# Sums of the keys' squares from two rounded parts, placed behind both query products, in a two-layer hybrid decoder kernel

## The reference, cut to what matters

```
def mla(c_q, c_kv, k_rope, ...):
    q = (rms_norm(c_q, cq_g) @ w_uq).reshape(b_, t_, MLA_HEADS, QK_HEAD)
    ckv = rms_norm(c_kv, ckv_g)
    k_nope = (ckv @ w_uk).reshape(b_, t_, MLA_HEADS, QK_NOPE)
    v = (ckv @ w_uv).reshape(b_, t_, MLA_HEADS, V_HEAD)
    k = jnp.concatenate([k_nope, k_r], axis=-1)
    q = rms_norm(q, qn_g)
    k = rms_norm(k, kn_g)          # needs the sum of k_nope's squares per head and token
    ... rope on the last 64 entries, causal softmax(q k) v
```

## Time and profile before

| what | us |
|---|---|
| median of three executions (range) | 1718.37 (1717.32 to 1718.63) |
| the profiled execution, its own time | 1717.03 |
| its span, first to last instruction | 1715.2 |
| PE busy (share of the span) | 1698.3 (99%) |
| PE weight loads | 1593.6 (93%) |
| POOL busy | 1203.0 (70%) |
| DVE busy | 892.2 (52%) |
| ACT busy | 484.9 (28%) |
| mean granted TensorE clock | 0.998 of full |

### The profile page before, as it was taken

The page is one execution under the profiler, slowest core; times in us unless marked ns, Lnnn a source line. Parts: engine busy times, 40 slices in busy tenths (PEclk is TensorE's granted clock), DMA queues, the critical chain, the costliest instruction groups (busy, mean ns, idle before and its releaser), DMA issues.

```text
span 1715.2 us, 32297 instructions
## 1 busy us (share of the span) xinstructions
PE 1698.3 (99%) x11976; PEld 1593.6 (93%) x11976; DVE 892.2 (52%) x1279; ACT 484.9 (28%) x867; POOL 1203.0 (70%) x1365
## 2 busy tenths in 40 slices
PE   7999999999999999999999999999999999999999
PEld 7999999999999999999999999999998888888887
DVE  7966758485545452212358757584856455322221
ACT  4423333332322331101134333333324223311110
POOL 7764848485688777777765748484857898777773
PEclk9999999999999999999999999999999999999999
DMA  4431222122232232232432313121222222322233
GB/s 158 139 98 62 92 72 81 65 92 86 87 110 74 86 123 100 86 98 86 162 116 76 107 59 98 60 92 66 92 86 98 98 86 86 139 96 98 88 121 112
DMA packets 49408, 164.23 MB, mean 96 GB/s; under 512 B 6048, under 2 KB 7456, under 8 KB 49056
## 3 DMA queue, kind: packets, MB, share of 16 engines
q1 hardware_dynamic: 41328, 146.56, 25.8%
q10 hardware_dynamic: 8032, 17.03, 3.0%
HBM read 152.21 MB, written 10.81 MB: 95 GB/s over the span
## 4 chain that ended last, share of the span: by engine, by line
PE 97%; DVE 1%; ACT 0%; issue 0%; ACTq 0%; POOL 0%; DVEq 0%; POOLq 0%
PE slots L507 85%; PE slots L572 3%; PE slots L605 3%; PE slots L667 2%; PE slots L590 1%; PE slots L541 1%; PE slots L557 1%; PE slots L575 0%; ACT residual_or_merged L955 0%; DVE sc_acc L1393 0%; DVE sc_acc L1397 0%; DVE residual_or_merged L1347 0%; PE slots L550 0%; DVE r_bias L1337 0%; DVE norm_diag L1103 0%
## 5 line engine op out<-in xcount | busy, mean ns | idle before, releaser
L419 POOL TENSOR_TENSOR w_lo<-w_raw,w_hi 128x256 fp32r<-128x256 f32 x1004 | 838.3, 865 | 20.9
L414 POOL TENSOR_SCALAR w_hi<-w_raw 128x1024 fp32r<-128x1024 f32 x251 | 289.5, 1154 | 337.0 <-PE slots L507 329.9
L507 PE MATMUL slots<-h_hi,w_hi 128*128 128x264 f32 (+1 forms) x2112 | 521.3, 311 | 0.0
L507 PE MATMUL slots<-h_lo,w_hi 128*128 128x264 f32 (+1 forms) x2112 | 515.6, 308 | 0.0
L507 PE MATMUL slots<-h_hi,w_lo 128*128 128x264 f32 (+1 forms) x2112 | 514.7, 308 | 0.0
L507 PEld LDWEIGHTS slots<-h_hi,w_hi 128*128 128x128 f32 x2112 | 342.7, 188 | 19.7
L507 PEld LDWEIGHTS slots<-h_hi,w_lo 128*128 128x128 f32 x2112 | 341.7, 188 | 19.1
L507 PEld LDWEIGHTS slots<-h_lo,w_hi 128*128 128x128 f32 x2112 | 342.0, 188 | 17.8
L507 PE MATMUL slots<-branch_hi,w_hi 128*128 128x264 f32 (+1 forms) x576 | 144.0, 313 | 10.5 <-DVE branch_lo L1109 8.7
L507 PE MATMUL slots<-branch_lo,w_hi 128*128 128x264 f32 (+1 forms) x576 | 142.9, 312 | 0.0
L507 PE MATMUL slots<-branch_hi,w_lo 128*128 128x264 f32 (+1 forms) x576 | 142.5, 311 | 0.0
(11 more groups left out here) (236 smaller groups left out, 2860.6 us busy)
## 6 DMA issues: line engine op xcount, KB each, us to landing
w_raw<-w_units SPq DMA_DIRECT2D x251, 512.0 KB, 3.3
stream<-sc_acc ACTq DMA_DIRECT2D x16, 264.0 KB, 2.1
sc_back<-stream SPq DMA_DIRECT2D x2, 2112.0 KB, 8.0
x_old<-stream SPq DMA_DIRECT2D x16, 264.0 KB, 4.3
stream<-residual_or_merged ACTq DMA_DIRECT2D x16, 264.0 KB, 2.4
ab_raw<-w_units SPq DMA_DIRECT2D x8, 512.0 KB, 4.2
residual_or_merged<-xt ACTq DMA_DIRECT2D x4, 528.0 KB, 7.9
stream<-xt ACTq DMA_DIRECT2D x1, 2112.0 KB, 9.5
```

The lines of the kernel that those rows point to most:

```text
L414: pool.tensor_scalar(hi, raw, 1.0, 1.0, ALU.mult, ALU.mult).then_inc(sem("hi_part"), 1)
L419: op = pool.tensor_tensor(lo[:, cols], raw[:, cols], hi[:, cols].bitcast(F32), ALU.subtract)
L507: mm = pe.matmul(out[:, a_, 0:t1 - t0], w(k), x(k)[:, t0:t1], start=(n == 0), stop=(n == 3 * ks - 1))
```

## The change

In the sums of the keys' squares the fp32 squares are replaced by a rounded hi part and a rounded lo part, and the matrix of ones by a rounded one (`ones_r`, made once). ACT squares each key twice, once into fp32 (`ct[4]`, `ct[5]`) and once rounded into `kn_hi`, which is not in use at that point; DVE subtracts to get the lo part in `kn_lo`. PE makes each sum from four fp32r matmuls where there were two fp32 ones. The sums stand behind both query products on PE; on ACT the square roots stand behind the queries' parts; on DVE the queries' lo parts stand ahead of the reading of the sums. `sc_input(0)` moves up on DVE, to the place between the keys' and the rotary lo parts. The gaps of filling k-tiles are dealt anew, 28 in place of 24 ahead of the first scores. Slots stay as they were. The new semaphores' entries and the making of `ones_r` on ACT at the start are left out of this diff.

```diff
@@ -71,7 +71,7 @@
 FILL = ("c0", "x0", "g0", "b0", "ga0", "c1", "x1", "g1", "b1", "ga1")
-FILLS = (8, 16, 4, 4, 4, 5, 5, 2, 6, 6, 7, 7, 6)
+FILLS = (8, 20, 4, 4, 3, 4, 5, 3, 5, 5, 6, 7, 6)
 STAGES = {"NORM": (1, 0, 0), "CQ": (1, 6, 2), "ATT": (4, 12, 0), "RG": (4, 8, 0), "MR": (4, 4, 0),
@@ -83,7 +83,7 @@
     "ATT": [("va", 2, "att_mm"), ("kn0", 0, "att_mm"), ("kn1", 1, "att_mm"), ("vb", 3, "unit_used"),
-            ("sum_k0", 0, "att_mm"), ("sum_k1", 1, "att_mm"), ("qn0", 2, "att_mm"), ("qn1", 3, "unit_used"),
+            ("qn0", 2, "att_mm"), ("qn1", 3, "unit_used"), ("sum_k0", 0, "att_mm"), ("sum_k1", 1, "att_mm"),
             ("qr", 1, "att_mm"), ("stat_q", 3, "att_mm"),
...
@@ -676,17 +677,26 @@
 
-                    for h in range(2):
-                        out = free("ATT", l, p, f"sum_k{h}")
-                        pe.wait_ge(*at("k_squared", l, p, h + 1))
-                        spread_sum(out, ct[h]).then_inc(sem("att_mm"), 1)
-
                     pe.wait_ge(*was_read("CQ", l, 0, "q2"))
                     hi, lo = unit_ready("ATT", l, p, 1)
-                    for h in range(2):
+
+                    def queries(h):
+
                         out = free("ATT", l, p, f"qn{h}")
...
                                 KQ).then_inc(sem("unit_used" if h else "att_mm"), 1)
+
+                    queries(0)
+                    queries(1)
+                    for h in range(2):
+                        out = free("ATT", l, p, f"sum_k{h}")
+                        pe.wait_ge(*at("k_sq_lo", l, p, h + 1))
+                        for a_ in range(2):
+                            cols = slice(a_ * HALF, (a_ + 1) * HALF)
+                            for n, squares in enumerate((kn_hi, kn_lo)):
+                                mm = pe.matmul(out[:, a_, 0:HALF], ones_r[:], squares[:, h, cols], start=(n == 0),
+                                               stop=(n == 1))
+                        mm.then_inc(sem("att_mm"), 1)
                     out = free("ATT", l, p, "qr")
@@ -824,6 +834,7 @@
             act.activation(ident_r[:], ident[0:TOK, 0:TOK], ACT.Copy).then_inc(sem("consts_ready"), 1)
+            act.activation(ones_r[:], ones[:], ACT.Copy).then_inc(sem("consts_ready"), 1)
             act.activation(causal_r[:], causal[0:TOK, 0:TOK], ACT.Copy).then_inc(sem("consts_ready"), 1)
@@ -888,24 +899,26 @@
                         act.wait_ge(*ready("ATT", l, p, f"kn{h}"))
-                        act.activation(halves(ct[h][:]), slot(slot_of("ATT", f"kn{h}")), ACT.Square).then_inc(
+                        act.activation(halves(ct[4 + h][:]), slot(slot_of("ATT", f"kn{h}")), ACT.Square).then_inc(
                             sem("k_squared"), 1)
+                        act.activation(halves(kn_hi[:, h, :]), slot(slot_of("ATT", f"kn{h}")), ACT.Square).then_inc(
+                            sem("k_sq_hi"), 1)
                         act.activation(halves(ct[2 + h][:]), slot(slot_of("ATT", f"kn{h}")), ACT.Identity, bias=zero,
...
                     for h in range(2):
-                        act.wait_ge(*was_read("ATT", l, p, f"sum_k{h}"))
-                        act.activation(ct[4 + h][:], ct[4 + h][:], ACT.Sqrt, bias=eps, scale=1.0 / QK).then_inc(
-                            sem("k_rms"), 1)
-
-                    for h in range(2):
                         act.wait_ge(*ready("ATT", l, p, f"qn{h}"))
...
                                        scale=hparam(l, QN_G)).then_inc(sem("q_hi"), 1)
+                    for h in range(2):
+                        act.wait_ge(*was_read("ATT", l, p, f"sum_k{h}"))
+                        act.activation(ct[4 + h][:], ct[4 + h][:], ACT.Sqrt, bias=eps, scale=1.0 / QK).then_inc(
+                            sem("k_rms"), 1)
+
                     act.wait_ge(*ready("ATT", l, p, "qr"))
@@ -916,6 +929,8 @@
                         act.wait_ge(*at("k_full", l, p, h + 1))
+                        if h == 0:
+                            act.wait_ge(*ready("ATT", l, p, "sum_k1"))
                         act.activation(kn_hi[:, h, :], ct[2 + h][:], ACT.Copy).then_inc(sem("k_hi"), 1)
@@ -1252,6 +1267,15 @@
                     for h in range(2):
+                        dve.wait_ge(*at("k_squared", l, p, h + 1))
+                        dve.wait_ge(*at("k_sq_hi", l, p, h + 1))
+                        lo_part(kn_lo[:, h, :], ct[4 + h][:], kn_hi[:, h, :], "k_sq_lo")
+                    for g in range(2):
+                        dve.wait_ge(*at("q_hi", l, p, g + 1))
+                        dve.scalar_tensor_tensor(halves(qn_lo[:, g, :]), slot(slot_of("ATT", f"qn{g}")),
+                                                 hparam(l, QN_G), halves(qn_hi[:, g, :]).bitcast(F32), ALU.mult,
+                                                 ALU.subtract).then_inc(freed("ATT", f"qn{g}"), 1)
+                    for h in range(2):
                         dve.wait_ge(*ready("ATT", l, p, f"sum_k{h}"))
@@ -1265,11 +1289,6 @@
                         k_inverse(g)
-
-                        dve.wait_ge(*at("q_hi", l, p, g + 1))
-                        dve.scalar_tensor_tensor(halves(qn_lo[:, g, :]), slot(slot_of("ATT", f"qn{g}")),
-                                                 hparam(l, QN_G), halves(qn_hi[:, g, :]).bitcast(F32), ALU.mult,
-                                                 ALU.subtract).then_inc(freed("ATT", f"qn{g}"), 1)
 
@@ -1300,9 +1319,17 @@
                                                      freed("ATT", "stat_q") if h else sem("q_ms"), 1)
+                    def sc_input(s):
+
+                        dve.wait_ge(*ready("ATT", l, p, f"x{s}"))
+                        dve.wait_ge(*was_read("ATT", l, p, f"c{s}"))
+                        dve.tensor_tensor(halves(s_pad[:, SCONV - 1:]), slot(slot_of("ATT", f"x{s}")),
+                                          halves(s_c[:]), ALU.mult).then_inc(freed("ATT", f"x{s}"), 1)
+
                     for h in range(2):
...
                         lo_part(kn_lo[:, h, :], ct[2 + h][:], kn_hi[:, h, :], "k_lo")
+                    sc_input(0)
                     for h in range(2):
@@ -1377,13 +1404,6 @@
 
-                    def sc_input(s):
-
-                        dve.wait_ge(*ready("ATT", l, p, f"x{s}"))
-                        dve.wait_ge(*was_read("ATT", l, p, f"c{s}"))
-                        dve.tensor_tensor(halves(s_pad[:, SCONV - 1:]), slot(slot_of("ATT", f"x{s}")),
-                                          halves(s_c[:]), ALU.mult).then_inc(freed("ATT", f"x{s}"), 1)
-
                     def sc_conv(s, m):
@@ -1418,7 +1438,6 @@
 
-                    sc_input(0)
                     for n in range(10):
```

More of the change, by code:

```diff
@@ L112 @@
     "rope_split": ("ATT", 1), "att_mm": ("ATT", 10),
-    "k_squared": ("ATT", 2), "v_hi": ("ATT", 2), "k_sum": ("ATT", 1), "k_rms": ("ATT", 2), "q_summed": ("ATT", 2), "k_rinv": ("ATT", 2), "k_full": ("ATT", 2), "kr_scaled": ("ATT", 2),
+    "k_squared": ("ATT", 2), "k_sq_hi": ("ATT", 2), "k_sq_lo": ("ATT", 2), "v_hi": ("ATT", 2), "k_sum": ("ATT", 1), "k_rms": ("ATT", 2), "q_summed": ("ATT", 2), "k_rinv": ("ATT", 2), "k_full": ("ATT", 2), "kr_scaled": ("ATT", 2),
     "k_hi": ("ATT", 2), "k_lo": ("ATT", 2), "krp_hi": ("ATT", 2), "krp_lo": ("ATT", 2),
@@ L215, in build @@
         ones = sb("ones", [P, P])
+        ones_r = sb("ones_r", [P, P], F32R)
         lane_consts = sb("lane_consts", [P, 2 + 2 * NTOK])
@@ L650, in _ @@
                     pe.wait_ge(sem("params_in"), 48)
-                    pe.wait_ge(sem("consts_ready"), 2)
+                    pe.wait_ge(sem("consts_ready"), 3)
                 with nc.Fori(0, PAIRS, engines=bass.OrderedEngineSet([pe.engine]), head_slot={pe.engine: 0}) as p:
```

## The result

| | before | after |
|---|---|---|
| median (range), us | 1717.84 (1715.89 to 1718.63) | 1821.76 (1821.02 to 1822.43) |
| span of the profiled execution, us | 1715.2 | 1820.1 |
| mean granted TensorE clock | 0.998 | 0.975 |

The change makes the kernel slower by 6.05%, ratio 1.0605 with a 95% interval of 1.0589 to 1.0621. The forecast was slower, 1737 us with a range of 1728 to 1749; the direction held, and the size was missed by 85 us.

A forecast was written before the change was run, and what follows sets the result against it. PE was taken to bound the kernel, with no slack. -7.4 + 0.8 + 20.6 + 4 = +18.0 us on 1717.03 gives 1735.0; 1736.4 for a median, plus half a microsecond for the clock: 1737, range 1728 to 1749.

The forecast's parts named there:

- PE's own work: Key sums on PE: eight fp32r matmuls take 0.98 us in place of 1.90, -0.92 a pass, -7.4 over eight.
- Anything that takes work off PE is gained whole: Premise: PE is busy 1698.3 of 1715.2 us, so saved work counts whole and new waits are lost whole.
- The wait for `vb`'s slot: Ahead of `qn1`: PE waits some 0.1 us a pass (0 to 0.3) for DVE's read, +0.8 over eight.
- The wait ahead of `qr`: PE waits for DVE to read `sum_k1` in the shared slot 1: 2.6 us a pass, 20.6 over eight.
- DVE's chain and the first scores: Normed keys begin 3.9 us later, at 264.9; PE reaches the first scores at 282.7, with no wait taken.
- the cover of 0.7 us: At the first scores, 28 filling k-tiles cover DVE's late chain by 0.7 us; upper end 5.6 us in all.
- The gaps between scores: Third gap loses one k-tile, 0.5 us wait at `turn`, +4 over eight (0 to 6); other shortened gaps have more to spare.
- The clock: Half a microsecond added to the sum for clock falls less frequent than in Rival 1.
- Rival 1: Clock falls in the new waits; a fall every pass adds 10 to 13 us, 1748; range 1742 to 1750, chance 0.22.
- Rivals 2 and 3: 2: POOL slows DVE's chain, scores wait too, 1743 to 1749, 0.08. 3: saving without the `qr` wait, 1713, faster 0.06.
- the same: No change in time, if the wait at `qr` were 0.9 to 1.3 us; chance 0.04.

The follow-up runs named there:

- e9_two28: e7_order with the first head's short convolution spread over later blocks and filling k-tiles dealt so x1 begins a block later, two-part sums kept: 1719.39 us, 1.0015.
- e8_single: The kernel before, order and dealing kept, with the keys' squares in one rounded part and no lo part: 1717.06 us, 0.9995.
- e1_fills24: The changed kernel with the old dealing of the filling k-tiles, 24 ahead of the first scores: 1746.37 us, 1.0172.
- e4_qr_slot2: The changed kernel with `qr` in slot 2 in place of slot 1: 1799.53 us, 1.0478.
- e6_gate_qr2: The changed kernel with both cures, the readers moved up as in e5_gate and `qr` in slot 2: 1732.19 us, 1.0085.
- e5_gate: The changed kernel with the gate's tanh and `sc_gate(0)` ahead of the first softmax, `sc_copy(1)` ahead of the sixth block's exponential: 1754.83 us, 1.0223.
- e2_only28: The kernel before with the new dealing of the filling k-tiles alone, 28 ahead of the first scores: 1802.17 us, 1.0498.
- e3_busy: The changed kernel with matmuls nobody reads put into PE's waits ahead of `qr`, `ga0` and `x1`: 1785.54 us, 1.0397.
- e12_deal25: The kernel before with fp32 sums, one filling k-tile moved ahead of the first scores, `sc_input(0)` earlier, first head's short convolution spread: 1718.12 us, 1.0008.
- e7_order: e6_gate_qr2 with the second query's lo part moved behind the first reciprocal on DVE: 1724.81 us, 1.0043.
- e11_single25s: e12_deal25 with squares in one rounded part, the second key's sum and `qr` in slot 2, `qn0` in slot 1: 1706.77 us, 0.9942.

## Why the prediction was wrong, step by step

- **PE's own work: right.** Two sums in eight matmuls, 279.38 to 280.36, 0.98 us against 1.90. Where nothing waits at `qr`, the saving is there: in e9_two28 PE reaches the queries' token sums 20.14 us after the pass's start (262.81 - 242.67), before 20.85 (264.44 - 243.59), which is 0.92 less some 0.2 of wait for `vb`'s slot. What it saved was lost later in the pass.
- **"Anything that takes work off PE is gained whole": wrong as a premise.** PE's list of waits shows no slack, but the chains of DVE and ACT stand right behind it. e8_single took 11.3 us of work off PE and gained 0.9.
- **The wait for `vb`'s slot: right in its place and in its range, twice the forecast in size.** DVE's read starts at 276.61; less the 24.70 us by which this pass is later than that of the earlier trace rows (its `qn0` starts at 274.80, the sums there at 250.10), 251.91, as forecast. `qn1` starts at 277.09, 2.29 us behind `qn0` where 18 matmuls take 2.19, and its first two matmuls are 0.23 apart, not 0.12: some 0.2 us, forecast 0.1 (0 to 0.3).
- **The wait ahead of `qr`: right.** Forecast 2.6 a pass and 20.6 in all, measured 2.5 and 20.1, ended by DVE's second reading of the sums.
- **DVE's chain and the first scores: right, on other grounds.** The normed keys began at 289.77 - 24.70 = 265.07 (forecast 264.9). The first scores came at 309.26 - 24.70 = 284.56 and not at 282.7, since the clock fall behind `qr` cost 1.7; they did not wait. Without that fall the cover of 0.7 us was thin: PE waits at the first scores in e1_fills24, e4_qr_slot2 and e6_gate_qr2. Rows of DVE after, whose last one shows 3.29 us idle ahead of the first row maximum:

```profile
281.59 1.31 DVE L1282 TENSOR_TENSOR early<-slots,residual_or_merged 128x528 f32<-128x528 f32 x2
...
289.77 1.11 DVE L1298 TENSOR_TENSOR early<-early 128x528 f32<-128x528 f32 x1
...
309.98 0.27 DVE L1361 TENSOR_REDUCE r_max<-slots 106x1 f32<-106x106 f32 x1 [3.29 <-PE slots L576]
```

- **The gaps between scores: the step that failed.** The forecast put +4 us there. I checked each shortened gap against the softmax chain, "the other shortened gaps have more to spare", and never asked which filling tile begins in each gap. The four k-tiles moved ahead make 32 done at the end of the first gap, so that `ga0` begins in the second; its slot 0 still holds `g0`, and DVE reads that (`sc_gate(0)`) only behind the second block's scaling. Before, `ga0` began one gap later. By the sixth block 48 are done, and `x1` begins before ACT's copy of `c1`, which stands behind the sixth exponential. The wait that I priced at 4 us, at the third `turn`, was hidden behind the one at `ga0`; it came out, at 4.8 us, when e5_gate took that away. In its place stood 26.6 + 23.7 = 50.3 us, which e2_only28 makes out of the dealing alone and e5_gate takes away down to 7.3.
- **The clock: the second term mis-sized, 0.5 us in the sum, 42 measured.** Rival 1 had the mechanism right and was given 0.22. I priced 10 to 13 us for a fall after eight waits. There were three waits a pass, and 42 us. Its price for one fall (1.3 to 1.6) was near the 1.71 measured. The evidence that I held against it, the idle gap of 1.77 us that passed without a fall, was one draw: of eight profiled executions with that gap (1.77 to 1.88 us), five had the clock at half within 5 us behind it, three did not.
- **Rivals 2 and 3 and "the same": did not occur.** The faster side needed the saving without the wait at `qr`; the wait was there.

Of the 85 us missed, some 46 are the two slot waits less the 4 at `turn`, and some 40 the clock, of which e2_only28 (mean 0.983, some 27 us more than before) shows that most goes with these two waits.

## What to carry to other kernels

Where independent work fills the gaps of a dependent chain, a new dealing has to be checked twice: against the chain that a gap covers, and against the reader of the buffer that each filling tile starts in. A tile's start moved by one gap put PE behind a reader queued after the very chain that it was to cover. And where the matmul engine is the bound, price a wait with the half clock that may follow it: here three waits of 2.5 to 3.6 us a pass cost 70 us as such and 42 us in clock.

## What the runs showed of the hardware that was not expected

- Matmuls whose result nobody reads made the kernel 36 us faster, since they kept the granted clock at 1.00 (mean 0.998 against 0.975) through waits that were filled and not shortened.
- The fall is not decided by the length of one wait. The same wait of 2.5 us ahead of `qr` was followed by half clock in seven of eight passes of the changed kernel, in three of eight with the old dealing (e1_fills24), and in three of eight with the new dealing but without the wait at `ga0` (e5_gate). An idle gap of 1.9 us near 18 us was followed by half clock in e3_busy, e5_gate, e6_gate_qr2, e8_single and e12_deal25, and by none in the kernel before, e2_only28 and e7_order. What else decides it stays open; no run here separates the time of the wait from the work around it.
- So two runs can differ by some us in clock alone (6.9 us lost in e12_deal25's profiled execution, 1.7 in e11_single25s's), and a difference of that size is to be read from passes at a clock of 1.00.
